# State-space blocks of a hybrid layer: transposed output product, tap products in column groups, the skip term in a diagonal, outer-product phases, and all elementwise work on VectorE

## What is computed

```python
v = ca * xa
ya = (ba * short_conv(v, conv_w) * silu(za)) @ proj_a       # convolution branch
for d in range(2):                                          # forward, backward
    h0 = last state of the scan over the context tokens
    x_re, x_im = scan(u @ b_bar, a, h0, reverse=(d == 1))   # 64 complex states in each of 64 groups
    y[d] = x_re @ c_re - x_im @ c_im                        # 16 channels in each group
y = gelu(y[0] + y[1] + ssm_d * u)                           # ssm_d * u is the skip term
```

## Time and profile before

| | |
|---|---|
| median of 3 runs | 2335.16 us (2334.63 to 2337.46) |
| profiled execution | 2332.53 us, its span 2330.6 us |
| TensorE busy | 2210.8 us (95%) |
| VectorE, ScalarE, GpSimd busy | 1048.0, 585.3, 428.4 us |
| mean granted TensorE clock | 0.959 of full speed |
| phase 1, from about 307 us to about 894 us |

### The profile page before, as it was taken

How to read it: one execution, slowest core, us unless ns; L and a number is a source line. 1 busy time by engine, 2 the same in 40 slices (tenths; PEclk the granted TensorE clock), 3 DMA queues, 4 the chain that set the end, 5 groups by cost and what they waited for, 6 DMA issues and landing times.

```text
span 2330.6 us, 27212 instructions
## 1 busy us (share of the span) xinstructions
PE 2210.8 (95%) x9865; PEld 1756.6 (75%) x9865; DVE 1048.0 (45%) x1404; ACT 585.3 (25%) x907; POOL 428.4 (18%) x442
## 2 busy tenths in 40 slices
PE   8879988889888898999999999999999999999997
PEld 1238877778777787888888888888868888888785
DVE  4340047677676774555533344443243333333224
ACT  0641132232222322222222222222212222222122
POOL 0043275557655560000000000000000000000000
PEclk9999998899888998999999999999999999999898
DMA  9962232232322324444433444444403333333233
GB/s 332 334 150 75 83 98 75 78 92 72 81 74 79 90 84 139 129 137 120 143 100 94 124 128 134 131 128 129 133 21 97 99 96 94 99 99 111 100 135 116
DMA packets 414879, 270.03 MB, mean 116 GB/s; under 512 B 52038, under 2 KB 383278, under 8 KB 413222
## 3 DMA queue, kind: packets, MB, share of 16 engines
q1 hardware_dynamic: 405608, 265.11, 37.3%
q10 hardware_dynamic: 9216, 4.20, 1.0%
HBM read 251.17 MB, written 18.09 MB: 116 GB/s over the span
## 4 chain that ended last, share of the span: by engine, by line
PE 70%; POOL 12%; issue 10%; DVE 4%; DMA 2%; SPq 1%; ACT 1%; ACTq 0%; POOLq 0%; DVEq 0%
PE ac L646 17%; PE ac L642 17%; PE ac L643 17%; POOL wlo L520 4%; PE ac L579 4%; PE ac L804 1%; PE ac L675 1%; PE ac L805 1%; PE ac L806 1%; POOL gph L537 1%; POOL PH L538 1%; PE ss L805 1%; PE ss L804 1%; PE ss L806 1%; PE ac L666 1%
## 5 line engine op out<-in xcount | busy, mean ns | idle before, releaser
L827 ACT ACTIVATE whi<-wslot 128x1024 fp32r<-128x1024 f32 x328 | 347.1, 1060 | 1499.3 <-PE ac L646 1093.4
L642 PE MATMUL ac<-hxh,whi 128*128 128x512 f32 x1664 | 660.0, 397 | 0.0
L643 PE MATMUL ac<-hxl,whi 128*128 128x512 f32 x1664 | 655.1, 394 | 0.0
L1381 DVE TENSOR_TENSOR wlo<-wslot,whi 128x1024 fp32r<-128x1024 f32 x246 | 301.4, 1226 | 648.5 <-ACT whi L827 648.5
L646 PE MATMUL ac<-hxh,wlo 128*128 128x512 f32 x1664 | 412.0, 390 | 2.8 <-POOL wlo L520 2.7
L642 PEld LDWEIGHTS ac<-hxh,whi 128*128 128x128 f32 x1664 | 318.3, 191 | 67.9 <-issue 1.9
L643 PEld LDWEIGHTS ac<-hxl,whi 128*128 128x128 f32 x1664 | 317.7, 191 | 65.8 <-issue 0.2
L646 PEld LDWEIGHTS ac<-hxh,wlo 128*128 128x128 f32 x1664 | 311.7, 188 | 70.3 <-POOL wlo L520 5.8
L520 POOL TENSOR_TENSOR wlo<-wslot,whi 128x1024 fp32r<-128x1024 f32 x82 | 207.9, 2545 | 300.1 <-ACT whi L827 299.0
L642 PE MATMUL ac<-bah,whi 128*128 128x512 f32 x384 | 149.5, 389 | 2.3 <-ACT whi L827 2.3
L643 PE MATMUL ac<-bal,whi 128*128 128x512 f32 x384 | 149.4, 389 | 0.0
(11 more groups left out here) (282 smaller groups left out, 2687.1 us busy)
## 6 DMA issues: line engine op xcount, KB each, us to landing
wslot<-w_in SPq DMA_DIRECT2D x224, 512.0 KB, 3.6
ring<-w_ada SPq DMA_DIRECT2D x32, 1024.0 KB, 7.6
gwt<-w_ada SPq DMA_DIRECT2D x128, 128.0 KB, 2.6
wslot<-w_out SPq DMA_DIRECT2D x32, 512.0 KB, 3.6
wslot<-proj_a SPq DMA_DIRECT2D x16, 512.0 KB, 3.9
wslot<-proj_b SPq DMA_DIRECT2D x16, 512.0 KB, 3.8
wslot<-proj_c SPq DMA_DIRECT2D x16, 512.0 KB, 3.8
xn<-x SPq DMA_DIRECT2D x4, 1024.0 KB, 12.7
```

The lines of the kernel that those rows point to most:

```text
L642: mm(ac[:, bank, :], w, xh, start=(v == 0 and q == 0), stop=False)
L643: mm(ac[:, bank, :], w, xl, start=False, stop=False)
L827: cp = lambda o, i, scale=1.0: nc.scalar.activation(o, i, ACT.Copy, scale=scale)
L1381: tt(wlo[:, s, :], wslot[:, s, :], whi[:, (U0[k] + j) % 2, :].bitcast(F32), ALU.subtract)\
```

## The change

All of it is in phase 1, and the matrix products are not touched.

1. Y is computed transposed: X or U (64 columns) is stationary, and M or Cp moves, 128 columns a matmul. The result, 64 chunks x 1024, is copied by ScalarE (`y_cols`), transposed back by eight small TensorE transposes (`y_back`, inside the next turn's first product) and copied once more (`y_rows`). One DMA stores it in place of eight.
2. The 16 tap products write into four column groups of one PSUM bank (partitions 0, 32, 64, 96), in turns.
3. The skip term is put into the tap of distance zero: a small diagonal `dd` is added to Tl. L1290 and L1357 go. The additions to Tl move ahead of the X operations.
4. PH becomes the product of two short tables, Elo (16) and Ehi (6), built once before the phase by `unit_phases`; each turn makes six VectorE operations of 128 x 768 of them.
5. VectorE makes all `wlo` of the phase; GpSimd does nothing in it.
6. V of the next turn, the turned table copies and the load of the table move to the end of the turn before.
7. ScalarE's copies to S are 12 in place of 24.

```diff
@@ product and TensorE's turn @@
                 last.then_inc(w_used, 1)
+                if mid is not None and v == 0:
+                    mid()
...
+        def y_back(b):
+            pe.wait_ge(yt_cp, 1)
+            pe.wait_ge(yt_cp, b)
+            for l in range(L):
+                last = tr(ss[:, 3, l * NX:(l + 1) * NX],
+                          yt[:, l * 128:(l + 1) * 128], ident[0:NX, 0:NX])
+            last.then_inc(yb_ps, 1)
...
-            product(1, b, 0, 2, 0, xs_of)
+            product(1, b, 0, 2, 0, xs_of, mid=None if first else (lambda: y_back(b)))
...
-            for d in range(2):
-                for g in range(GB):
+            for n in range(4):
+                for dq in range(4):
+                    d, g = dq // 2, 4 * (dq % 2) + n
...
-                    last = mm(ss[0:H, 2 * d + g // 4, (g % 4) * 128:(g % 4 + 1) * 128],
+                    last = mm(ss[32 * dq:32 * dq + H, 0, n * 128:(n + 1) * 128],
                               V[:, d, g, at0:at0 + H], Cp[:, d, g, cp0:cp0 + L * H], start=True, stop=True)
...
-                o = ss[:, 0, g * NX:(g + 1) * NX]
-                mm(o, M[:, g, :], U[:, g, NC:NQ], start=True, stop=False)
-                mm(o, Cp[:, 0, g, H:(L + 1) * H], X[:, 0, g // 2, g % 2, :], start=False, stop=False)
-                last = mm(o, Cp[:, 1, g, 0:L * H], X[:, 1, g // 2, g % 2, :], start=False, stop=True)
+                o = ss[0:NX, g // 4, (g % 4) * 128:(g % 4 + 1) * 128]
+                mm(o, U[:, g, NC:NQ], M[:, g, :], start=True, stop=False)
+                mm(o, X[:, 0, g // 2, g % 2, :], Cp[:, 0, g, H:(L + 1) * H], start=False, stop=False)
+                last = mm(o, X[:, 1, g // 2, g % 2, :], Cp[:, 1, g, 0:L * H], start=False, stop=True)
@@ ScalarE's turn @@
+            if not first:
+                y_cols(b)
             hi(1, b, 2)
+            if not first:
+                y_rows(b)
             hi(1, b, 3)
...
+            if not (isinstance(b, int) and b == NB - 1):
+                turned_tables(b + 1)
             hi(1, b, 8)
@@ VectorE's turn, in its new order @@
             dve.wait_ge(v_done, b + 1)
+            if dyn or b:
+                dve.wait_ge(y_ps, b)
...
             link(last)
+            lo(1, b, 2)
...
             last.then_inc(cp_done, 1)
+            lo(1, b, 3)
             dve.wait_ge(cp_done, b + 1)
-
+            phases(b)
+            tt(dd[:, :, :], ident[0:H, 0:H].unsqueeze(1).to_broadcast([H, GB, H]),
+               dtab[0:H, sl(b, GB)].unsqueeze(2).to_broadcast([H, GB, H]), ALU.mult)
+            lo(1, b, 4)
             dve.wait_ge(w_used, b * 8 + (U0[1] + 4))
             freed(dve, 1, b, 0)
             tt(cv[:, :], ac[:, 1, :], xas[:, :], ALU.mult).then_inc(ac_free[1], 1)
...
+            lo(1, b, 5)
             dve.wait_ge(s_cp, 2 * b + 2)
-            dve.wait_ge(ph_done, b + 1)
...
+            lo(1, b, 6)
             for ri in range(2):
...
             link(last)
+            lo(1, b, 7)
+            dve.wait_ge(t_cp, b + 1)
+            for q in range(2):
+                o = dd[:, 4 * q:4 * q + 4, :]
+                last = tt(o, o, ss[32 * q:32 * q + H, 0, :].rearrange("p (g c) -> p g c", g=4)[:, :, 0:H], ALU.add)
+            link(last)
+            o = Tl[:, :, 112:128]
+            tt(o, o, dd[:, :, :], ALU.add).then_inc(t_add, 1)
             w = slice(NC - 1, NQ - 1)
...
             last.then_inc(x_done, 1)
-
...
+            dve.wait_ge(x_done, b + 1)
+            more = dyn or b < NB - 1
+            if more:
+                state_mults(b + 1)
+            lo(1, b, 8)
+            if more:
+                state_adds()
+            lo(1, b, 9)
             dve.wait_ge(w_used, b * 8 + (U0[1] + 8))
```

More of the change, by code:

```diff
@@ L88, in repeat @@
     for (c, per), s in zip(counts, starts):
-        c.n = s + n * per
+        c.n = s + (n - tail) * per
+    for i in range(n - tail, n):
+        body(i)
 def sl(i, size):
@@ L409, in y_store @@
         def y_store(b):
[L410 to L415, removed]
+            if not isinstance(b, int):
+                sp.compute_val(b * (T * 4))
+            sp.wait_ge(yb_cp, b + 1)
+            sp.dma_start(y_dram[:, bass.ds(b * T, T)], yo[:, :]).then_inc(y_out, 16)
         sp.wait_ge(bb_done, 1)
@@ L521, in lo @@
                 .then_inc(w_lo, 1)
[L524 to L549, removed]
         for j in range(2):
@@ L903, in conv_turn, with y_cols, y_rows @@
             last.then_inc(bc2, 1)
+        def y_cols(b):
+            act.wait_ge(y_ps, b)
+            cp(yt[:, :].rearrange("c (l g h) -> c g l h", g=GB, l=L),
+               ss[0:NX, 0:2, :].rearrange("c q (g l h) -> c (q g) l h", l=L, h=H)).then_inc(yt_cp, 1)
+        def y_rows(b):
+            act.wait_ge(yb_ps, b)
+            if not (isinstance(b, int) and b == 1):
+                act.wait_ge(y_out, b * 16 - 16)
+            cp(yo[:, :], ss[:, 3, :]).then_inc(yb_cp, 1)
+        def conv_turn(b):
+            first = isinstance(b, int) and b == 0
+            if not first:
+                y_cols(b)
             hi(1, b, 2)
+            if not first:
+                y_rows(b)
             hi(1, b, 3)
@@ L953, in conv_turn @@
             a(sg[:, :], ac[:, 3, :], ACT.Sigmoid).then_inc(sig_done, 1)
-        repeat(act, NB, conv_turn, peel=1)
+        turned_tables(0)
+        repeat(act, NB, conv_turn, peel=1, tail=1)
+        y_cols(NB)
+        y_rows(NB)
         act.wait_ge(cp_done, NB)
@@ L1252, in powers, with lo, unit_phases @@
             return tt(tmp, bi, w2, ALU.mult), o
-        def conv_turn(b):
-            dyn = not isinstance(b, int)
+        def lo(k, i, j):
+            u, s, _ = unit(k, i, j)
+            dve.wait_ge(w_hi, u + 1)
+            tt(wlo[:, s, :], wslot[:, s, :], whi[:, (U0[k] + j) % 2, :].bitcast(F32), ALU.subtract)\
+                .then_inc(w_lo, 1)
+        def unit_phases():
+            tmp = S[:, :, :, :, :].rearrange("p a d l c -> p (a d l c)")
+            for E, lev0, count in ((Elo, 0, 16), (Ehi, 4, NQ // 16)):
+                v.memset(E[:, 0, :, 0:1].rearrange("p m c -> p (m c)"), 1.0)
+                link(v.memset(E[:, 1, :, 0:1].rearrange("p m c -> p (m c)"), 0.0))
+                n, lev = 1, lev0
+                while n < count:
+                    m = min(n, count - n)
+                    pr, pi = (w[:, lev, :].unsqueeze(2).to_broadcast([128, 64, m]) for w in (PWr, PWi))
+                    er, ei_ = E[:, 0, :, 0:m], E[:, 1, :, 0:m]
+                    ta, tb = (tmp[:, q * 512:q * 512 + 64 * m].rearrange("p (a m) -> p a m", m=m) for q in range(2))
+                    tt(E[:, 0, :, n:n + m], er, pr, ALU.mult)
+                    tt(E[:, 1, :, n:n + m], er, pi, ALU.mult)
+                    tt(ta, ei_, pi, ALU.mult)
+                    link(tt(tb, ei_, pr, ALU.mult))
+                    tt(E[:, 0, :, n:n + m], E[:, 0, :, n:n + m], ta, ALU.subtract)
+                    link(tt(E[:, 1, :, n:n + m], E[:, 1, :, n:n + m], tb, ALU.add))
+                    n, lev = n + m, lev + 1
@@ L1256, in conv_turn, with state_mults @@
+        def state_mults(b):
             dve.wait_ge(bc2, b + 1)
-            if dyn or b:
+            if not (isinstance(b, int) and b == 0):
                 dve.wait_ge(k_ps, b)
-                dve.wait_ge(y_ps, b)
             for d in range(2):
@@ L1376, in _ @@
             cpy(bah[:, n, :], src).then_inc(hs_done, 1)
-        def lo(k, i, j):
-            u, s, _ = unit(k, i, j)
-            dve.wait_ge(w_hi, u + 1)
-            tt(wlo[:, s, :], wslot[:, s, :], whi[:, (U0[k] + j) % 2, :].bitcast(F32), ALU.subtract)\
-                .then_inc(w_lo, 1)
         def gate_tile(br, i, r):
```

126 lines of the change are left out of this document (64 added, 62 removed).

## The result

The changed kernel takes 2205.55 us (median of 4 runs, 2201.26 to 2208.25) where the kernel before takes 2336.18: a ratio of 0.9439, interval 0.9423 to 0.9456. It is faster by 5.6%, 131 us, where 101 were forecast. The profiled execution took 2205.15 us, with a span of 2203.4.

What follows compares the result with a forecast made beforehand. Bound: TensorE's wait for M and the low clock behind it in phase 1. Seven periods 86.8 us, first turn 8, end 6: 101 us off 2332.5 gives 2231.7, forecast 2234; range 2227 to 2248, 0.85 between 2214 and 2266.

Steps and rivals of the forecast that it cites:

- What bounds the kernel: Phase 1: TensorE waits 6.8 us for M each turn, then Y takes 10.2 us at granted clock 0.50.
- TensorE's sum: TensorE's own work in a phase 1 turn: products, transposes, S, taps and Y, 59.7 us in all.
- M's chain: From the second product's end: `t_add` at +21.0 us, M at +28.5, before TensorE needs it at +29.3.
- The scans 6.05: VectorE's scans in a phase 1 turn, on the way to `t_add`, taken as 6.05 us.
- the rival of the side-by-side groups: Tap column groups run in parallel in phase 1: a turn of 57.5 to 59 us, 2217 to 2227; chance 0.12.
- VectorE's way round: VectorE's work in a turn from `t_add` to readiness for cv: 37.2 to 42.5 us, against TensorE's 38.7.
- The `lo` in time: Each `wlo` on VectorE: 6.9 us remain between two for other work; it fits or misses by a fraction.
- What is hidden: `unit_phases`, near 20 us, lies in VectorE's idle time before 317 us; copies, store and table load are off the path.
- VectorE as the bound: Rival: VectorE's high operation lengths hold in phase 1, a turn of 63.5 us, 2260 us in all; chance 0.22.
- the low clock in Y: Rival: Y stays at clock 0.50 and takes 10.2 us, a turn of 65.8 us, 2281 in all; chance 0.09.
- slower: Rival: twelve VectorE phase and Z operations all take 3.155 us, VectorE's turn 84 us, 2419 in all; chance 0.05.
- no change: Rival: the wait comes back in full in another place, for instance `wlo` late in several units; chance 0.01.

Runs made afterwards that it cites:

- Moving one block: The kernel before with only the small additions to Tl moved ahead of the X operations on VectorE: 2284.7 us, ratio 0.9793.
- the experiment with one group: The changed kernel with the 16 tap products written to partitions 0 to 15 of four banks, as before: 2224.7 us, ratio 0.9541.

## Why the prediction was right in kind and short in size

The profiled executions differ by 2332.5 - 2205.2 = 127.4 us, their spans by 127.2; the sum had said 100.8. Item by item:

| | forecast | measured |
|---|---|---|
| seven periods | 7 x (72.4 - 60.0) = 86.8 | 506.76 - 399.22 = 107.5 |
| up to the first Y | 8 | 377.5 - 367.9 = 9.7 |
| last Y to the merge's second product | 6 | 25.05 - 18.25 = 6.8 |
| behind that | 0 | 3.2 |

The last row is not the change's: the two traces lie 124.0 us apart at the merge and still at the Fourier stage, and the rest appears in the output projection, where the kernel before ran some matmuls at the low pace that the changed one ran at the full one. The four runs of the changed kernel differ by up to 7 us.

*What bounds the kernel* held, by experiment: M's lateness came from VectorE's order, and the idleness made the low clock. Moving one block removed both.

*TensorE's sum*, 59.7, is the step that failed: "Taps 3.6 if the column groups bring nothing". I kept the upper bound as the value. Measured: 1.09, so 2.5 us a turn too much, 20 us in all; the experiment with one group puts 19 to 24 us on it. `y_back` cost 0.64 us and no visible switch, where 1.1 were set. Y at 5.4 (5.43) and products at 11.1 (10.8 to 11.2) were right.

*M's chain* had a second oversize that would have hidden the first: "The scans 6.05". The row stood beside a `wlo` of GpSimd, as L1307's did; I had taken that company out of L1307 and left it in the scans. Alone they take 4.09. With 6.05, M would have come at +29 and TensorE, at +26.6, would have waited for it; the rival of the side-by-side groups was priced so. So the turn of 57.0 needed both terms to be smaller than forecast. `t_add` came at +19.0 (forecast +21.0), the S copies took 4.2 (4.5).

*VectorE's way round* was early, even beyond the low end (35.8 us from `t_add` to readiness for cv, 37.2 forecast): Cp products 1.35 (not the 1.16 that the prediction worked out), V products 1.22, phase operations 0.95. It is idle for 5.8 us in a turn (2.8, 1.4, 1.6). *The `lo` in time*: right, in the changed kernel. *What is hidden*: right in the main, the first V starts at 318.8 us (317.1 before).

*The rivals.* The side-by-side groups, at 0.12, is the case that occurred; its price of 57.5 to 59 us a turn was above the 57.0 measured, so the range ended too high. VectorE as the bound, the low clock in Y, slower, and no change did not occur. The low clock's condition was right: with 5 us or more of idleness back, the experiments show it, and the old orientation then costs the most.

## What to carry to other kernels

Where one engine's short wait is followed by a slow stage, look for the small operation that feeds the wait and stands behind large ones in its queue: moved ahead, it removes the wait and the low clock behind it, and then the next engine in line must be relieved too. Small products with few stationary columns are cheap when their outputs lie in different column groups: 3.3 times for four groups of 16 columns, 1.95 times for two of 64. A duration read beside another engine's operation is not the operation's own; take the least one of its group, for every term of the sum alike.

## What the runs showed of the hardware that was not expected

Behind 5.1 to 6.8 us of idleness, a stage of 24 float32 matmuls with 128 stationary and 64 moving columns stayed at 0.43 us a matmul to its end (10.2 us), in all 16 turns of two kernels, although TensorE was busy all the time. The same stage with 64 stationary and 128 moving columns left the low pace about 4.5 us in. With no more than 1.2 us of idleness ahead both ran at 1.00, in 5.26 and 5.43 us. Why the orientation matters stays open.

Idleness is not all that goes before a low clock. In the output projection of the kernel before, TensorE had no gap from 2139 to 2167 us, and yet over eight small float32 products with `ones` stationary the pace halved at about 2160 us: the granted clock is 0.55 from 2160.1 to 2163.7 and 0.50 behind it. The changed kernel shows the same at 2047.9 us.

And the column groups gave their speed without any loss seen at their two borders with full-width products.
